# Last tiles of each feed-forward stage turned inside the preceding product, and new step orders at seams and in a mixer

## The reference, cut to what matters

```python
# layers 0 and 1
x = layer_norm(ALPHA * x + mixer(x))
x = layer_norm(ALPHA * x + square(relu(x @ w_up)) @ w_down)          # hidden width 4096
x = x + sigmoid(x @ ple_w_gate + b) * (p @ ple_w_proj)
# second block
h = h + 0.5 * (silu(n(h) @ wg) * (n(h) @ wu)) @ wd                    # n = rmsnorm, hidden width 2816
h = h + concat(rmsnorm(nsa(n(h))), rmsnorm(fox(n(h)))) @ w_out
h = h + 0.5 * (silu(n(h) @ wg2) * (n(h) @ wu2)) @ wd2
h = h + sigmoid(n(h) @ ple_w_gate) * rmsnorm(p @ ple_w_proj)
```

## Time and profile before

| | us |
|---|---|
| runs of the kernel, median of three | 1263.57 (1262.92 to 1265.23) |
| profiled execution, its own time | 1265.18 |
| its span, first to last instruction | 1263.5 |
| PE busy | 1209.6 |
| DVE busy | 745.6 |
| ACT busy | 619.0 |

### The profile page before, as it was taken

The page is one execution under the profiler, slowest core; times in us unless marked ns, Lnnn a source line. Parts: engine busy times, 40 slices in busy tenths (PEclk is TensorE's granted clock), DMA queues, the critical chain, the costliest instruction groups (busy, mean ns, idle before and its releaser), DMA issues.

```text
span 1263.5 us, 14900 instructions
## 1 busy us (share of the span) xinstructions
PE 1209.6 (96%) x5837; PEld 996.5 (79%) x5837; DVE 745.6 (59%) x981; ACT 619.0 (49%) x923; POOL 40.4 (3%) x61
## 2 busy tenths in 40 slices
PE   7999999999999889999989999999999899999998
PEld 6887788887777778888877888877878777888876
DVE  5668654556775575454577545456976455445536
ACT  5454444444455444344346444445786565444445
POOL 1000000000000000000001000000111010000000
PEclk9999999999999899999999999999999999999999
DMA  8545565654643345545535556553651326565540
GB/s 305 170 175 167 183 200 167 200 193 142 215 175 104 106 167 184 184 166 205 192 115 185 182 184 198 173 179 103 193 197 34 109 89 208 187 193 176 179 152 34
DMA packets 119510, 210.71 MB, mean 167 GB/s; under 512 B 8256, under 2 KB 66832, under 8 KB 119440
## 3 DMA queue, kind: packets, MB, share of 16 engines
q1 hardware_dynamic: 119440, 209.75, 50.0%
HBM read 208.68 MB, written 1.05 MB: 166 GB/s over the span
## 4 chain that ended last, share of the span: by engine, by line
PE 86%; DVE 7%; ACT 4%; issue 1%; DMA 1%; POOL 0%; SPq 0%; DVEq 0%; ACTq 0%
PE psum L313 26%; PE psum L315 25%; PE psum L314 25%; PE psum L1316 2%; DVE wl L294 2%; PE psum L448 2%; PE psum L1284 2%; ACT wh L284 1%; PE psum L1303 1%; DVE xT_low L706 1%; PE psum L749 1%; ACT xT_high L729 1%; DMA x<-in_x 1%; PE psum L1287 0%; DVE neg_max L1354 0%
## 5 line engine op out<-in xcount | busy, mean ns | idle before, releaser
L265 DVE TENSOR_TENSOR wl<-ring,wh 128x2048 fp32r<-128x2048 f32 x132 | 302.6, 2292 | 274.6 <-ACT wh L257 274.6
L313 PE MATMUL psum<-wh,xT_high 128*128 128x512 f32 (+4 forms) x1008 | 401.0, 398 | 17.2 <-DVE xT_low L706 7.9
L315 PE MATMUL psum<-wh,xT_low 128*128 128x512 f32 (+4 forms) x1008 | 390.2, 387 | 0.0
L314 PE MATMUL psum<-wl,xT_high 128*128 128x512 f32 (+4 forms) x1008 | 389.3, 386 | 0.0
L257 ACT ACTIVATE wh<-ring 128x2048 fp32r<-128x2048 f32 x132 | 252.7, 1914 | 231.8 <-PE psum L315 231.8
L313 PEld LDWEIGHTS psum<-wh,xT_high 128*128 128x128 f32 x1008 | 190.6, 189 | 58.5 <-issue 12.0
L315 PEld LDWEIGHTS psum<-wh,xT_low 128*128 128x128 f32 x1008 | 190.1, 189 | 38.5
L314 PEld LDWEIGHTS psum<-wl,xT_high 128*128 128x128 f32 x1008 | 190.7, 189 | 34.1
L313 PE MATMUL psum<-wh,hidT_high 128*128 128x512 f32 (+1 forms) x520 | 200.9, 388 | 8.1 <-DVE hidT_low L583 6.6
L314 PE MATMUL psum<-wl,hidT_high 128*128 128x512 f32 (+1 forms) x520 | 198.3, 383 | 0.0
L315 PE MATMUL psum<-wh,hidT_low 128*128 128x512 f32 (+1 forms) x520 | 198.2, 383 | 0.0
(11 more groups left out here) (279 smaller groups left out, 924.1 us busy)
## 6 DMA issues: line engine op xcount, KB each, us to landing
ring<-in_mlp_w_up SPq DMA_DIRECT2D x32, 1024.0 KB, 5.3
ring<-in_mlp_w_down SPq DMA_DIRECT2D x32, 1024.0 KB, 4.9
ring<-in_ffn_wg SPq DMA_DIRECT2D x44, 512.0 KB, 3.9
ring<-in_ffn_wu SPq DMA_DIRECT2D x44, 512.0 KB, 4.9
ring<-in_ffn_wd SPq DMA_DIRECT2D x22, 1024.0 KB, 5.0
ring<-in_ple_w_gate SPq DMA_DIRECT2D x12, 1024.0 KB, 5.2
ring<-in_w_in SPq DMA_DIRECT2D x10, 1024.0 KB, 5.2
ring<-in_a_w_in SPq DMA_DIRECT2D x8, 1024.0 KB, 9.7
```

What stands on the lines that cost most here:

```text
L265: K.nc.vector.tensor_tensor(K.wl[:, n % PARTS, 0:w], K.ring[:, n % SLOTS, 0:w], K.wh[:, n % PARTS, 0:w].bitcast(F32), ALU.subtract).then_i ...
L313: nc.tensor.matmul(out, x[0], w[0], start=start, stop=False)
L314: nc.tensor.matmul(out, x[0], w[1], start=False, stop=False)
L315: return nc.tensor.matmul(out, x[1], w[0], start=False, stop=stop)
```

## The change

In `feed_forward` the last chunk's `turn_hidden`, with ACT's and DVE's "parts" for it, goes into the product of the chunk before it. In the MLP stages it stands halfway in `down(6)`. In the gated stages it stands behind the two t=0 pieces of chunk 9, and the piece (9, t=1, 0), so far the tail's first step, is made right behind it. For ACT and DVE "parts" of the last chunk now comes before the split of the load two behind `down_load(count - 2)`'s last.

```diff
@@ -400,10 +400,13 @@
         for c in range(count):
             if c + 1 < count:
                 yield from [("split", up_load(c + 1)), ("hidden", c + 1, 0)]
-            yield ("parts", c)
+            if c + 1 < count:
+                yield ("parts", c)
             if c + 1 < count:
                 yield from [("split", up_load(c + 1) + 1), ("hidden", c + 1, 1)]
             for i in range(nd):
+                if c == count - 2 and i == nd - 1:
+                    yield ("parts", c + 1)
                 if down_load(c) + i + 1 < first + total:
                     yield ("split", down_load(c) + i)
 
@@ -491,6 +494,8 @@
 
         def down(c):
             for j in range(jt):
+                if c == count - 2 and j == jt // 2:
+                    turn_hidden(c + 1)
                 n = down_load(c) + j * nd // jt
                 if j % (jt // nd) == 0:
                     weights_here(K, pe, n)
@@ -511,12 +516,14 @@
         for c in range(count):
             if c + 1 < count:
                 up(c + 1, 0)
-            turn_hidden(c)
-            if c + 1 < count:
+                turn_hidden(c)
                 up(c + 1, 1)
             if c == count - 1 or gated and c == count - 2:
                 for j in range(jt):
                     down_piece(c, 0, j)
+                    if c == count - 2 and j == jt - 1:
+                        turn_hidden(c + 1)
+                        down_piece(c, 1, 0)
             else:
                 down(c)
```

The nine seams and the second block's mixer get new orders of the same steps, except that the gated tails lose `down 9 0`. After ffn1:

```diff
...
-    yield "down", 9, 0
-    yield "down", 9, 1
     yield "update", 0, 0
...
     yield "turn", 0, 1
+    yield "down", 9, 1
     yield "down", 10, 0
     yield "down", 10, 1
+    yield "high", 0, 0
+    yield "square", 0, 0
+    yield "square", 0, 1
+    yield "high", 0, 1
     yield "lead_high", 1, 0
-    yield "high", 0, 0
-    yield "high", 0, 1
     yield "low", 0, 0
...
     yield "lead_high", 1, 1
-    yield "square", 0, 0
-    yield "square", 0, 1
+    yield "update", 1, 0
     yield "lead_low", 1, 0
+    yield "update", 1, 1
     yield "lead", 0
-    yield "update", 1, 0
-    yield "update", 1, 1
     yield "lead_low", 1, 1
...
     yield "turn", 1, 1
-    yield "square", 1, 0
     yield "high", 1, 0
...
     yield "high", 1, 1
+    yield "square", 1, 0
     yield "square", 1, 1
```

In the mixer's list about half of the lines change place. The stretch that the prediction speaks of:

```diff
...
         yield "zturn", 0, 0
...
+        yield "values", 19
+        yield "values", 20
         yield "turn", 21
-        yield "values", 19
-        yield "scores", 23
-        yield "values", 20
         yield "tiles", 4
-        yield "keep", 22
         yield "tiles", 5
         yield "values", 21
+        yield "low", 19, 0
         yield "tiles", 6
         yield "tiles", 7
-        yield "low", 19, 0
+        yield "keep", 22
         yield "turn", 22
+        yield "scores", 23
         yield "out", 0, 0, 0
...
```

More of the change, by code:

```diff
@@ L970, in after_mlp_1 @@
     yield "copy", 1, 0
+    yield "copy", 1, 1
     yield "high", 0, 1
-    yield "copy", 1, 1
+    yield "normal", 0, 1
+    yield "update", 1, 0
+    yield "low", 0, 0
     yield "lead_low", 1, 0
-    yield "update", 1, 0
     yield "update", 1, 1
     yield "stats", 1, 0
+    yield "lead_low", 1, 1
     yield "low", 0, 1
     yield "stats", 1, 1
-    yield "lead_low", 1, 1
     yield "spread", 1
@@ L999, in after_embed_0 @@
     yield "logit", 0
+    yield "gate", 0, 0
+    yield "turn", 0, 0
+    yield "sigmoid", 0
+    yield "gated", 0
+    yield "low", 0, 0
     yield "lead_low", 0, 0
-    yield "turn", 0, 0
-    yield "gate", 0, 0
-    yield "sigmoid", 0
     yield "lead_low", 0, 1
-    yield "gated", 0
     yield "gate", 0, 1
@@ L1086, in after_ffn1, with after_nsa @@
     yield "lead_high", 1, 1
-    yield "square", 0, 0
+    yield "update", 1, 0
+    yield "lead_low", 1, 0
+    yield "update", 1, 1
+    yield "lead", 0
+    yield "lead_low", 1, 1
+    yield "turn", 1, 0
+    yield "turn", 1, 1
+    yield "high", 1, 0
+    yield "low", 1, 0
+    yield "low", 1, 1
+    yield "high", 1, 1
+    yield "square", 1, 0
+    yield "square", 1, 1
+    yield "lead", 1
+def after_nsa():
+    yield "last", 2, 0
+    yield "update", 0, 0
+    yield "update", 0, 1
+    yield "last", 2, 1
+    yield "turn", 0, 0
+    yield "turn", 0, 1
+    yield "last", 3, 0
+    yield "last", 3, 1
+    yield "lead", 0
+    yield "square", 0, 0
+    yield "high", 0, 0
+    yield "high", 0, 1
+    yield "lead_high", 1, 0
+    yield "low", 0, 0
+    yield "low", 0, 1
+    yield "lead_high", 1, 1
     yield "square", 0, 1
+    yield "update", 1, 0
     yield "lead_low", 1, 0
-    yield "lead", 0
-    yield "update", 1, 0
     yield "update", 1, 1
@@ L2186, in steps @@
+        yield "hidturn", 0
         yield "high", 14, 0
         yield "keep", 6
-        yield "dense", 3, 1, 1, range(2, 4)
+        yield "values", 3
+        yield "keep", 7
+        yield "hidturn", 1
         yield "hidT", 0
-        yield "keep", 7
-        yield "hidturn", 0
-        yield "hidturn", 1
+        yield "take", 3, 1
+        yield "group", 0
+        yield "high", 14, 1
         yield "hidT", 1
-        yield "high", 14, 1
-        yield "shares", 1
-        yield "turn", 6
@@ L2197, in steps @@
-        yield "take", 3, 1
-        yield "cw2",
-        yield "scores", 8
-        yield "values", 4
-        yield "keep", 8
+        yield "keep", 8
+        yield "turn", 6
+        yield "scores", 8
+        yield "cw2",
+        yield "values", 4
+        yield "high", 15, 0
+        yield "low", 14, 0
+        yield "shares", 1
+        yield "high", 15, 1
+        yield "values", 5
         yield "dense", 4, 0, 0, range(2)
-        yield "low", 14, 0
-        yield "high", 15, 0
-        yield "high", 15, 1
+        yield "turn", 7
@@ L2242, in steps @@
-        yield "values", 9
-        yield "dense", 4, 1, 0, range(2, 4)
         yield "turn", 11
         yield "scores", 14
+        yield "keep", 13
+        yield "values", 9
+        yield "dense", 4, 1, 1, range(2)
+        yield "turn", 12
+        yield "norm", 3
         yield "values", 10
-        yield "keep", 13
-        yield "norm", 3
-        yield "dense", 4, 1, 1, range(2)
+        yield "scores", 15
+        yield "take", 4, 0
+        yield "values", 11
         yield "keep", 14
-        yield "turn", 12
@@ L2279, in steps @@
-        yield "values", 14
+        yield "dense", 5, 0, 1, range(2)
+        yield "keep", 16
+        yield "keep", 17
+        yield "turn", 16
+        yield "values", 14
+        yield "scores", 18
         yield "scores", 19
+        yield "turn", 17
+        yield "high", 18, 0
         yield "keep", 18
-        yield "turn", 17
+        yield "group", 3
+        yield "gain", 4
         yield "values", 15
-        yield "group", 3
         yield "dense", 5, 0, 1, range(2, 4)
-        yield "gain", 4
@@ L2356, in steps @@
         yield "scores", 28
-        yield "keep", 28
         yield "turn", 27
         yield "scores", 29
-        yield "values", 25
         yield "out", 0, 1, 0
+        yield "keep", 28
         yield "out", 0, 1, 1
+        yield "turn", 28
         yield "values", 26
+        yield "high", 20, 0
+        yield "values", 27
+        yield "out", 1, 1, 0
+        yield "low", 20, 0
+        yield "high", 20, 1
+        yield "turn", 29
+        yield "keep", 29
         yield "shares", 6
-        yield "turn", 28
@@ L2384, in steps @@
+        yield "turn", 30
+        yield "high", 21, 0
+        yield "shares", 7
+        yield "values", 28
         yield "values", 29
```

374 lines of the change are left out of this document (161 added, 213 removed).

## The result

The changed kernel takes **1245.57 us** (median of 4 runs, 1243.55 to 1247.28), beside 1264.38 for the kernel before in the same session: ratio 0.9852, 95% interval 0.9832 to 0.9872, so 18.8 us faster. The profiled execution took 1247.28 (span 1245.6) against 1265.18 (span 1263.5), 17.9 us less where the terms made 13.4.

The account below looks back on a forecast made before the run. TensorE bounds the kernel (busy 1209.6 of 1263.5 us), so only its idle time or slow stretches could pay. Terms 2.4 + 2.5 + 2.1 + 2.8 + 1.8 + 0.8 + 1.0 = 13.4 us; forecast 1251.0 us, range 1246 to 1259.

Parts of the forecast that it names:

- Turn, ungated, 2 x 1.07: Last turn in the two ungated feed-forward stages: waits on hidT_low of 1.07 us each go, 2.1 us gained.
- Turn and tail at ffn1, 2.4: First gated stage's end: 2.1 us from the turn, 1.7 of clock, less 1.5 idle in the tail; 2.4 taken.
- ffn2, 2.5: Second gated stage's turn and tail: 2.5 us gained, though `turn 1 0` would wait 1.65 instead of 0.78 for ScalarE's copies.
- mlp_1, 2.8: Seam behind the second ungated stage: lead 1 moves before the turn that waited for x; 2.8 us gained, 1.7 of it clock.
- nsa, 1.8: Seam behind the nsa mixer: reordered steps let the next stage start at 1042.35 instead of 1044.14, 1.8 us gained.
- Early seams, 0.25 net: Seams behind mlstm, the sinks mixer, mlp_0 and embedding 0: small gains and losses netting to 0.25 us.
- The mixer, 1.0: Second block's mixer, 345 steps not followed singly: 1.0 us gain taken, bounded by 5.6 idle and one 1.7 half-clock stretch.
- A: Whole kernel: the forecast itself, all terms paying as summed, 1251 us; chance 0.55.
- B: Whole kernel: half-clock falls stay or move, three stretches (5.1 us) come back, 1256 us; chance 0.2.
- C: Whole kernel: only the moved turns pay and the new orders net to nothing, 6 us gained, 1258 us; chance 0.12.
- D: Slower: in the mixer, weight splits placed before their buffers are free hold later steps in program order, 1267 us; chance 0.07.
- E: Same time: the turn comes no earlier, waiting for the second half-tile of hidden values, 1263 us; chance 0.06.

Follow-up runs that it names:

- e5: The changed kernel as it is, run again for a second sample of times and clocks: 1244.60 us, ratio 0.9845.
- e4: The kernel before with nine discarded 128x512 matmuls added in each gated stage's wait for hidT_low: 1262.62 us, ratio 0.9991.
- e15: The changed kernel with the old orders behind mlstm, the sinks mixer, mlp_0 and embedding 0: 1245.98 us, ratio 0.9865.
- e6: The changed kernel with the old step order of the second block's mixer: 1246.05 us, ratio 0.9854.
- e12: The changed kernel with the old order behind the second embedding (embedding 1): 1245.34 us, ratio 0.9857.
- e1: The kernel before with only the feed-forward edit (moved turns in all four stages), old seam and mixer orders: 1253.55 us, ratio 0.9927.
- e9: The kernel before with discarded matmuls in seven of TensorE's waits: 1258.31 us, ratio 0.9956.
- e8: The changed kernel with down piece 9, second half, put back first behind the first gated stage: 1244.52 us, ratio 0.9844.
- e13: The changed kernel with the old step order in ffn1's tail, its turn staying moved: 1243.28 us, ratio 0.9840.
- e3: The kernel before with only the new orders of the seven ungated seams, feed-forward and mixer as before: 1254.84 us, ratio 0.9933.
- e2: The kernel before with only the new step order of the second block's mixer: 1259.20 us, ratio 0.9967.

## Why the prediction was right and wrong

**Split of the 17.9 us between the profiles.** A 3.4 us fall costs 1.5 to 1.6 where TensorE is bound (S2: 154.18 against 152.60 in e5; S9: 50.8 against 49.2 in e4) and 3.15 for the 6.8 us one (S3: 167.97 against 164.81). In other places it costs less or as much: 0.45 for the one at 121 us with the new order behind mlstm (91.2 against 90.75 from VectorE's 61st instruction on), and in the mixer 1.1 at 971.3, 1.3 at 969.5 (e15) and 1.6 to 1.7 at 973 and 974 (e6, e12); that of before, at 983.2, cost 0.9, which is e6's 1.6 less the 0.75 by which the two traces close up there. Forecast: three falls gone, 5.1. Found: three gone (4.9); one moved from where it costs 1.6 to where it costs 0.45; one new, 1.6; the mixer's 0.2 dearer. That is about 4.2. Another 0.6 is the start of the kernel, which varies by itself. The work is then 13, and there the terms without their clock make only 8.3. The parts measured one by one add up to it: turns 1.3 + 1.3, the end of ffn1 1.2 (1.4 at lead 1, 1.0 over S7 and S8), ffn2 1.6, mlp_1 1.5, embedding 1 0.7, nsa 2.0, early seams 1.3, mixer 2.3, together 13.2.

- *Turn, ungated, 2 x 1.07*: 1.22 and 1.30 (S3 in e1 against before; S5, 67.38 in e1 against 68.68 in e9), nearly right.
- *Turn and tail at ffn1, 2.4*: lead 1 starts at 857.91, 17.65 us behind the last activation, against 868.82 and 20.64 before: 3.0, with 1.6 of clock. The step "PE idles 1.3 and then 0.2: 1.5 us lost" was wrong as a cost (e8). With the old tail order it is 3.7 (e13).
- *ffn2, 2.5*: 3.2, half of it clock. The wait of 1.65 for ScalarE's copies did not come; it stayed at 0.78, now for x. The start was worked out from durations laid end to end, and overlap between engines' steps was under-counted.
- *mlp_1, 2.8*: nearly right, 3.05, with its clock share; the work 1.5 against 1.1. *nsa, 1.8*: nearly right, 2.0. *embedding 1, 0.55*: 0.7, hidden in the profile by the new fall. *Early seams, 0.25 net*: 1.3. The "loss" behind the sinks mixer is a gain of 0.1.
- *The mixer, 1.0*: **the step that failed most**, 2.3. The forecast opens with the statement that only what shortens TensorE's idle time or its slow stretches can pay, and it bounded the mixer's gain by the 5.6 us idle in its rows and a fall. That took busy time as fixed because the instructions are. Idle time shrank by 0.9 only; 1.4 came out of short waits that the overlapping rows count as busy (e6). The value inside the bound, 1.0, was an analogy with the seams.

So the mechanism of A held, but its sum was 5 us of work too small, and the time lies outside the range for that. B's falls came, but fewer than went; C is refuted by e3 and e6, D by the result and e2, E by e1. That the clock's share came near the forecast is partly luck: which falls a run has varies, and those at 133 and 667 were not counted. The range's low end took 4 to 5 us from the mixer's bounds alone, less than the 6.3 that these bounds left (5.6 and 1.7, less the 1.0 taken), and nothing from the other terms, which came out 0.1 to 1.1 larger, all in one direction.

## What to carry to other kernels

Compare two kernels at equal granted clock, or by stretches between fixed marks, before explaining a difference of a few us: a half-speed stretch can leave or enter code that was not touched. Waits of 2.2 and 2.9 us cost TensorE more than their length in seven of eleven cases here, some 1.6 us each, and discarded matmuls in them can be worth placing, if they fall inside the wait and not behind it. When a step order is all that changes, a profile's busy time isn't a floor, as rows that overlap hide short waits: look at the time from one start to the next. In this case terms worked out with durations laid end to end came out too small throughout.

## What was not expected of the hardware

The granted clock fell behind waits of 2.2 and 2.9 us in seven of eleven cases, behind one of 1.7 for weights in three of ten, behind none of five of 2.5 at that same place, and behind groups of shorter ones (0.84 and 0.90 at 420 us), in some executions and not in others of the same program; its mean ran from 0.993 to 0.998 for the changed kernel and its time with it, from 1247.3 to 1242.9 us. A fall of 3.4 us cost 1.5 to 1.6 us in a feed-forward stage and 0.45 to 1.7 in other places. Behind nine 128x512 matmuls placed in each gated wait no fall came, in four cases. The same 941 TensorE instructions of the mixer were busy 155.5 us in one order and 152.5 in another; 1.6 of that is clock and 1.4 waits that overlapping rows hide.
